# Sliding-window attention on one core: a head's two half bands added before the turn and parted again by masks on the way out of PSUM

## What is computed

```python
diff = qi - (ku - BLK)                       # query minus key
band = (diff >= 0) & (diff < WINDOW)         # 0 <= q - k < 128
s = jnp.where(mask, s, -jnp.inf)
mx = jnp.maximum(jnp.max(s, axis=-1, keepdims=True), sink)
p = jnp.exp(s - mx)
p = p / (jnp.sum(p, axis=-1, keepdims=True) + jnp.exp(sink - mx))
o = jnp.einsum('bnhgqk,bnkhd->bnqhgd', p, vc)
return o.reshape(B, S, Hq * dh) @ w_out + b_out
```

## Time and profile before

| | us |
|---|---|
| median of 3 runs | 1095.64 (1095.62 to 1095.84) |
| the profiled execution | 1096.03 |
| its span, first to last instruction | 1094.2 |
| TensorE busy in the span | 1085.9 (99%) |
| VectorE busy | 534.9 (49%) |
| ScalarE busy | 429.0 (39%) |
| GpSimd busy | 53.7 (5%) |

### The profile page before, as it was taken

One profiled execution on the slowest core, in us unless ns is written; L12 is line 12 of the kernel. 1 busy time (PEld: TensorE's weight loads), 2 busy tenths in 40 slices (PEclk: granted clock), 3 DMA queues, 4 the chain that ended last, 5 costly groups with the idle time before them and its releaser, 6 DMA issues.

```text
span 1094.2 us, 14764 instructions
## 1 busy us (share of the span) xinstructions
PE 1085.9 (99%) x5558; PEld 910.8 (83%) x5558; DVE 534.9 (49%) x797; ACT 429.0 (39%) x750; POOL 53.7 (5%) x52
## 2 busy tenths in 40 slices
PE   9999999999999999999999999999999999999997
PEld 7888888898888888888889987789888888888886
DVE  7544578644444434333366587664343434523344
ACT  6511456543232323222355377653333232422242
POOL 1000211000000000000002024200000000000000
PEclk9999999999999999999999999999999999999999
DMA  8342327223323242122272542022323333312231
GB/s 273 107 119 77 116 81 228 72 72 88 114 77 115 77 115 77 39 96 96 96 193 59 153 99 77 2 77 80 113 83 109 87 105 90 101 38 96 96 134 77
DMA packets 141765, 109.51 MB, mean 100 GB/s; under 512 B 22481, under 2 KB 127089, under 8 KB 141729
## 3 DMA queue, kind: packets, MB, share of 16 engines
q1 hardware_dynamic: 140720, 105.84, 32.6%
q0 software_dynamic: 864, 2.92, 0.9%
q10 hardware_dynamic: 144, 0.26, 0.1%
HBM read 106.87 MB, written 2.13 MB: 100 GB/s over the span
## 4 chain that ended last, share of the span: by engine, by line
PE 93%; DVE 3%; ACT 2%; DMA 1%; issue 0%; SPq 0%; POOL 0%; DVEq 0%; ACTq 0%; POOLq 0%
PE ps L1491 17%; PE ps L1492 17%; PE ps L1493 17%; PE ps L1741 7%; PE ps L1742 7%; PE ps L1743 7%; PE ps L1686 3%; PE ps L1688 3%; PE ps L1687 3%; PE ps L1575 1%; PE ps L1577 1%; PE ps L1576 1%; PE ps L1865 1%; PE ps L1847 1%; PE ps L1834 1%; PE ps L1641 1%
## 5 line engine op out<-in xcount | busy, mean ns | idle before, releaser
L1491 PE MATMUL ps<-act_hi,w_hi 128*128 128x512 f32 (+1 forms) x1016 | 368.3, 363 | 0.1
L1492 PE MATMUL ps<-act_lo,w_hi 128*128 128x512 f32 (+1 forms) x1016 | 366.4, 361 | 0.0
L1493 PE MATMUL ps<-act_hi,w_lo 128*128 128x512 f32 (+1 forms) x1016 | 366.4, 361 | 0.0
L1491 PEld LDWEIGHTS ps<-act_hi,w_hi 128*128 128x128 f32 x1016 | 191.7, 189 | 31.2 <-DVE w_lo L929 0.9
L1493 PEld LDWEIGHTS ps<-act_hi,w_lo 128*128 128x128 f32 x1016 | 191.7, 189 | 28.9
L1492 PEld LDWEIGHTS ps<-act_lo,w_hi 128*128 128x128 f32 x1016 | 191.8, 189 | 28.8
L1741 PE MATMUL ps<-w_hi 128*128 128x512 f32 x288 | 112.0, 389 | 0.0
L1742 PE MATMUL ps<-w_lo,w_hi 128*128 128x512 f32 x288 | 112.0, 389 | 0.0
L1743 PE MATMUL ps<-w_hi,w_lo 128*128 128x512 f32 x288 | 112.0, 389 | 0.0
L757 ACT ACTIVATE arena<-ps,vecs 128x512 f32<-128x512 f32 x44 | 34.3, 779 | 188.6 <-PE ps L1493 188.6
L1257 DVE SCALAR_TENSOR_TENSOR arena<-ps,vecs,arena 128x511 f32<-128x511 f32 x44 | 33.0, 749 | 144.5 <-ACT arena L757 144.4
(11 more groups left out here) (210 smaller groups left out, 1224.3 us busy)
## 6 DMA issues: line engine op xcount, KB each, us to landing
raw<-in_f_w_up SPq DMA_DIRECT2D x88, 512.0 KB, 4.7
raw<-in_f_w_down SPq DMA_DIRECT2D x44, 512.0 KB, 3.2
raw<-in_m_w_in SPq DMA_DIRECT2D x23, 512.0 KB, 4.5
raw<-in_m_w_out SPq DMA_DIRECT2D x8, 512.0 KB, 3.2
raw<-in_a_w_in SPq DMA_DIRECT2D x16, 256.0 KB, 4.4
raw<-in_a_w_out SPq DMA_DIRECT2D x16, 256.0 KB, 4.8
h<-in_x SPq DMA_DIRECT2D x4, 512.0 KB, 7.4
h<-in_x_turned SPq DMA_DIRECT2D x3, 512.0 KB, 7.9
```

The costliest lines, as they stand in the source:

```text
L1491: nc.tensor.matmul(dst, uh[:, k], zh, start=(k == 0), stop=False)
L1492: nc.tensor.matmul(dst, uh[:, k], zl, start=False, stop=False)
L1493: ins = nc.tensor.matmul(dst, ul[:, k], zh, start=False, stop=(k == KT - 1))
```

## The change

In blocks 1 to 3 GpSimd first adds the previous block's half of each head to its own half, then multiplies the 128 columns by the inverse. TensorE turns 128 columns per head, step s to bank 2 + s % 2. VectorE (`unfold`) takes the turned tile out of PSUM twice: masked with `causal` < 0 as the previous block's part and with `causal` = 0 as its own. ScalarE copies only in block 0. The mix, and the even scores that reuse the banks, wait for VectorE's semaphore `own_done`. TensorE's third piece of filling moves behind both turns and the turn of the normed block. ScalarE does the exponentials before the copies. VectorE unfolds after the norms and before `inverse(2m+2)`; in pair 2 one split stands before the unfolding, one after it, and two behind `inverse(6)`.

```diff
-            for s in range(AT_STEPS):
-
-                b, lo = s % 4, P if s < ASTEPS else 0
+            def fold(s):
+
+                b = s % 4
                 pool.wait_ge(inv_done, s + 1)
-                nc.gpsimd.tensor_tensor(sc[:, b, :, lo:], sc[:, b, :, lo:],
-                                        asm[:, b, 5].unsqueeze(2).to_broadcast([P, AG, 2 * P - lo]),
+                own = sc[:, b, :, P:]
+                if s >= ASTEPS:
+                    nc.gpsimd.tensor_tensor(own, own, sc[:, b, :, 0:P], ALU.add).then_inc(pf_done, 1)
+                    pool.wait_ge(pf_done, s - ASTEPS + 1)
+                nc.gpsimd.tensor_tensor(own, own, asm[:, b, 5].unsqueeze(2).to_broadcast([P, AG, P]),
                                         ALU.mult).then_inc(pn_done, 1)
...
             def turned(s):
 
-                b, blk = s % 2, s // ASTEPS
                 act.wait_ge(pt_mm, s + 1)
-                lo = P if blk == 0 else 0
-                nc.scalar.copy(p_t[:, b, :, lo:], ps[:, 2:4].rearrange("p a (j k) -> p (a j) k", k=2 * P)
-                               [:, :, lo:]).then_inc(pt_done, 1)
+                nc.scalar.copy(p_t[:, s % 2, :, P:], ps[:, 2 + s % 2].rearrange("p (j k) -> p j k", j=AG))\
+                    .then_inc(pt_done, 1)
...
-                for s in (2 * m, 2 * m + 1):
-                    turned(s)
-                    if s + 2 < AT_STEPS:
-                        probs(s + 2)
+                if m + 1 < A_PAIRS:
+                    probs(2 * m + 2)
+                if 2 * m < ASTEPS:
+                    for s in (2 * m, 2 * m + 1):
+                        turned(s)
+                if m + 1 < A_PAIRS:
+                    probs(2 * m + 3)
...
+            def unfold(s):
+
+                dve.wait_ge(pt_mm, s + 1)
+                own_keys = causal[:].unsqueeze(1).to_broadcast([P, AG, P])
+                both = ps[:, 2 + s % 2].rearrange("p (j k) -> p j k", j=AG)
+                nc.vector.scalar_tensor_tensor(p_t[:, s % 2, :, 0:P], own_keys, 0.0, both, ALU.is_lt, ALU.mult)
+                nc.vector.scalar_tensor_tensor(p_t[:, s % 2, :, P:], own_keys, 0.0, both, ALU.is_equal, ALU.mult)\
+                    .then_inc(own_done, 1)
...
                 if m == 2:
-                    for k in range(4, KT):
-                        split_lo(G_AOUT + k)
+                    split_lo(G_AOUT + 4)
                 for w in pair_work(m, "post") + pair_work(m, "pre"):
                     work(w)
+                if 2 * m >= ASTEPS:
+                    for s in (2 * m, 2 * m + 1):
+                        unfold(s)
+                if m == 2:
+                    split_lo(G_AOUT + 5)
                 if m + 1 < A_PAIRS:
                     inverse(2 * m + 2)
+                if m == 2:
+                    for k in range(6, KT):
+                        split_lo(G_AOUT + k)
...
                 if s % 2:
                     if s >= 3:
                         pe.wait_ge(mx_done, s - 1)
+                elif s >= 2 * ASTEPS:
+                    pe.wait_ge(own_done, s - 2 - ASTEPS)
                 elif s >= 3:
                     pe.wait_ge(pt_done, s - 2)
...
                 pe.wait_ge(pn_done, s + 1)
-                if s % 2:
-                    pe.wait_ge(pt_done, s)
-                elif s + 2 < AT_STEPS:
+                if s % 2 == 0 and s + 2 < AT_STEPS:
                     pe.wait_ge(mx_done, s + 3)
                 for j in range(AG):
-                    for kb in range(1 if blk == 0 else 0, 2):
-                        ins = nc.tensor.transpose(ps[:, 2 + j // 2, ((j % 2) * 2 + kb) * P:
-                                                     ((j % 2) * 2 + kb + 1) * P],
-                                                  sc[:, b, j, kb * P:(kb + 1) * P], ident[:])
+                    ins = nc.tensor.transpose(ps[:, 2 + s % 2, j * P:(j + 1) * P], sc[:, b, j, P:], ident[:])
                 ins.then_inc(pt_mm, 1)
...
-                pe.wait_ge(pt_done, 2 * m + 2)
+                if blk == 0:
+                    pe.wait_ge(pt_done, 2 * m + 2)
+                else:
+                    pe.wait_ge(own_done, 2 * m + 2 - ASTEPS)
...
                 turn_probs(2 * m)
-                filling(m, 2)
                 turn_probs(2 * m + 1)
                 for w in pair_work(m, "turn"):
                     work(w)
+                filling(m, 2)
                 filling(m, 3)
```

More of the change, by code:

```diff
@@ L257, in trunk @@
         pn_done = sem("pn_done")
+        pf_done, own_done = sem("pf_done"), sem("own_done")
         qb_mm = sem("qb_mm")
@@ L540, in _ @@
                                         ALU.subtract).then_inc(w_lo_done, 1)
-            for s in range(AT_STEPS):
-                b, lo = s % 4, P if s < ASTEPS else 0
+            def fold(s):
+                b = s % 4
                 pool.wait_ge(inv_done, s + 1)
-                nc.gpsimd.tensor_tensor(sc[:, b, :, lo:], sc[:, b, :, lo:],
-                                        asm[:, b, 5].unsqueeze(2).to_broadcast([P, AG, 2 * P - lo]),
+                own = sc[:, b, :, P:]
[3 more added lines that the diff above has]
+                nc.gpsimd.tensor_tensor(own, own, asm[:, b, 5].unsqueeze(2).to_broadcast([P, AG, P]),
                                         ALU.mult).then_inc(pn_done, 1)
+            for m in range(A_PAIRS):
+                for s in (2 * m, 2 * m + 1):
+                    fold(s)
         @block.scalar
```

## The result

The changed kernel takes 1099.15 us (median of 9 executions, 1097.24 to 1099.78) against 1095.81 for the one before (9 executions): ratio 1.0025, 95% interval 1.0017 to 1.0034. It is slower by 3.3 us at the medians; the forecast said 2.6. Its executions form two groups: two lie at 1097.24 and 1097.52, seven at 1098.31 to 1099.78. The profiled one took 1097.52 and so belongs to the lower group; its span is 1095.7, 1.5 us more than the span before. So the profile holds only about half of the loss. What makes the other half, the experiments show in part.

The account below looks back on a forecast made before the run. TensorE was taken to bound the kernel; its 6.6 us saving would be lost to VectorE's longer chain, 2.1 us late at mix(6) plus 0.5 in pair 7: +2.6 on 1095.64, forecast 1098.2 us, range 1090.5 to 1103.0.

Parts of the forecast that it names:

- What bounds the kernel: Whole kernel: TensorE, busy 99% of the span, so only work leaving its queue gains and only making it wait costs.
- TensorE's part: Attention stage: fewer turns save 5.3 us, grouped turns 1.0, block 0's wait for ScalarE's copy 0.25; together 6.6 us.
- the change of work: TensorE switching between turns and products: one switch less per pair saves 0.13 us, 1.0 us over eight pairs.
- ScalarE's part: Twelve 128x1024 copies out of PSUM go, worth nothing by themselves; 14.9 us of waits at L1396 vanish; ScalarE never late.
- VectorE's part: Blocks 1 to 3: two masked products per step at 0.60 us each, 2.4 us per pair, 14.4 us in all.
- GpSimd's part: Add plus multiply take 2.3 to 2.4 us per step, 0.5 more; not on the path by length, but through collisions.
- The collision: VectorE instructions with both inputs in SBUF and GpSimd's exclude each other: 2.3 us in pair 2, 2.3 at seven other places.
- VectorE's chain: Pairs 2 to 6: 50.7 us of work plus waits and collisions put mix(6) at 704.85, 2.1 us later than before.
- Pair 7: Mix(6) to mix(7) takes 10.35 us against 9.85, 0.5 more, including up to 1.5 us for folding meeting the pre norm.
- 1: Attention stage: collisions between VectorE and GpSimd stay small, giving 1094.5 us, no visible change; chance 0.2.
- 2: Attention stage: VectorE doesn't bind, giving 1092.0 us, at the very best 1089.0; chance 0.22.
- 3, the clock: TensorE's clock may fall to 1.2 GHz behind a stall; with 5 us of it, 1103 us; chance 0.08.

Follow-up runs that it names:

- the early add: Changed kernel with GpSimd's add waiting for the exponentials instead of the inverse, so only the multiply is set off by the inverse; median 1098.77 us, ratio 1.0024.
- Covering the long stall: Changed kernel with eight products nobody reads in TensorE's queue ahead of the turns of step 6; median 1098.12 us, ratio 1.0017.
- then four: Changed kernel with unread products inside four TensorE stalls: step 6's turns, pair 5's even scores, a normed block's first turn, mix(6); median 1097.75 us, ratio 1.0017.

## Why the prediction came out as it did

**What bounds the kernel**: right. TensorE's queue bound it, and once nobody is late the saving there shows in the time: 6.15 us against 6.6 worked out.

**TensorE's part**: the turns right (12 x 0.44 = 5.3; measured 0.87 per pair, 5.2), the change of work wrong. The turn that waited for ScalarE's copy gave more than its 0.25: pair 0, from 628.84 before, went from 7.62 us to 7.18. I read 3.04 - 2.81 = 0.23 out of differences between products of different neighbours and took 0.13 per pair; it is 0.02. And the step had the wrong sign where it mattered. Moving the filling takes 1.4 us of cover from three waits (the pre norm, the folding of step 15 and the scores of step 12 are the stalls that went with the move back). I priced two of these waits without setting them against the move: the pre norm in pair 5 and the folding in pair 7. With the filling back the kernel is 2.7 us faster. The move was the cheapest thing in the diff to undo and I had booked it as a gain of 1.0.

**ScalarE's part**: right. It is busy 35.09 us of the 58, and no instruction of TensorE waited for it in the changed kernel.

**VectorE's part**: right. 680 ns and 0.60 apart, as the row of L1013 had it.

**GpSimd's part**: right in length (1.3 and 1.04 us), wrong in weight. I called the 0.5 us per step "not on the path by length" and priced the collisions at 4.6 us up to mix(6) and 1.5 in pair 7. They cost VectorE 5.6 and 0.5, and the mix(7) of the kernel without the add comes 5.2 us earlier.

**The collision**: right in kind. In pair 2 the splits and the folding took turns. Their price was 1.1 us at the splits and 0.85 at the inverse behind them, 2.0 against 2.3, since GpSimd's multiply met the small L1405 rather than a third split. The seven small ones: I took 2.3. L1396 and L1405 lost 4.5 together, and 3.6 of them without that 0.85; all seven in full I had summed to 4.6. Halving them "because a phase a few tenths away removes most of one" had no row behind it. The phases didn't drift apart: each inverse of an odd step sets off GpSimd or finds it at work, and the first L1396 of the pair comes 1.7 to 2.7 us behind it, every time into one of GpSimd's instructions (the multiply in pairs 3 and 6, an add in pairs 2, 4 and 5).

**VectorE's chain**: right at its end, in part by luck. Scores of pair 2 at 645.65, measured 645.48; maxima of step 8 about 665, measured 664.64; mix(6) at 704.85, measured 704.62. Inside, two terms make up for each other: the collisions up to there were 5.6 us (1.1 + 3.1 + 1.4) where I had 4.6, work and waits together 1 us less than worked out.

**Pair 7**: 10.35 us worked out, 9.78 measured. The folding of step 15 found the pre norm in its way, as forecast, for 0.66 us of TensorE's time and not 1.5. With that the profile's mix(7) lies at 714.40 and not 715.2: +1.8 by the chain where I said +2.6.

**The rivals.** 1 and 2 were wrong for the changed kernel; 2 describes the kernels without masks or add. 3, the clock, was priced at 1103 with a chance of 0.08, as a thing that either rules all executions or none. It is real and small: 1.6 us behind one stall in the trace of the early add. The Trainium skill's page "TensorE: Matmul & The Clock Gate", section "Part 1: The HAM clock gate", has the rule that the array falls back after idling; two traces agree, with 0.50 behind 1.96 us of idle and behind 2.57. One doesn't show it: the changed kernel's own, where 2.57 us of idle left the clock at 1.00.

So the median, 1099.15 against a forecast of 1098.2, is +1.8 us of the chain and some +1.6 us between the two groups of executions. The forecast had the chain at +2.6 and nothing for the groups. That the sum came near is luck: the first was overrated by 0.8 and the second left out.

The chain's part is shown. It comes from three things together: undoing any one of them (the masks, the add, the move of the filling) brings the time to that of the kernel before or under it. The part between the groups is shown only so far: the clocks recorded with the changed kernel's executions part the groups without an exception, and two other kernels' traces hold such a fall, one of them behind the same stall. Covering the long stall, and then four, took 0.7 and 1.0 us off the median. But no trace of the changed kernel's upper group exists, and a second group at full clock stayed when the long stall was covered. By these two runs I estimate that the clock makes half of the 1.6 us or somewhat more. What makes the rest stays open.

## What to carry to other kernels

Where one engine works without a gap, taking work off it gains only as long as every helper keeps its distance: count how many microseconds of cover stand between each producer and its wait before moving work across it, and set a gain of tenths against the cover it takes. Work put on GpSimd can cost VectorE time where it meets VectorE's instructions with both inputs in SBUF, even if GpSimd is busy for only 6% of the span as here. Moving that work in time may only change whom it meets. A stall can cost more than its length, in some executions only; so look at the spread of the executions and their clocks before believing a single profile.

## What the runs showed of the hardware

- VectorE and GpSimd take turns where both have instructions waiting that read two tiles in SBUF: two splits on VectorE and one folding's add and multiply on GpSimd interleaved as some 1.1, 1.2, 1.1 and 0.9 us, from 657.52 to 661.84. An instruction of 128x4 values, 0.15 to 0.16 us by itself, lasted up to 1.02 us (1.24 with the early add). Instructions with one input in PSUM kept their length beside GpSimd (0.69 us at 709.99).
- TensorE's granted clock went to 0.50, the 1.2 GHz level, for some 3 us behind 1.96 us of idle in one execution and behind 2.57 in another, and stayed at 1.00 behind 2.57 in a third.
- An add of two real tiles of 128x512 takes GpSimd 1.27 to 1.31 us where VectorE doesn't hold it up, a multiply by a broadcast column 1.04.
- Separating eight turns into two groups of four, with six products between, costs TensorE 0.02 us (10.44 against 10.42 us for a pair).
